# Eighteen units of w2 loaded by expert in 32 KB rows and multiplied two experts at a time, with the last steps rearranged

## The reference

```python
def moe(x, router_w, router_b, w1, b1, w2, b2):
    ...
    acc = jnp.zeros_like(xt)
    for e in range(N_EXPERTS):                      # 32
        gu = xt @ w1[e] + b1[e]                     # (288, 1024) @ (1024, 2048)
        gate = jnp.minimum(gu[:, :D_FF], SWIGLU_LIMIT)
        lin = jnp.clip(gu[:, D_FF:], -SWIGLU_LIMIT, SWIGLU_LIMIT)
        glu = gate * jax.nn.sigmoid(SWIGLU_ALPHA * gate)
        out = (glu * (lin + 1.0)) @ w2[e] + b2[e]   # (288, 1024) @ (1024, 1024)
        acc = acc + combine[:, e:e + 1] * out       # combine: top 4 of 32, else zero
    return acc.reshape(shp)

y_prompt = rmsnorm(hp, final_norm_g)
y_sample = rmsnorm(hs, final_norm_g)
```

## Time and profile before

| | |
|---|---|
| Median of three runs | 1020.77 us (1020.28 to 1022.32) |
| Profiled execution | 1020.11 us |
| Its span, first to last instruction | 1018.4 us |
| PE busy | 950.4 us (93%) |
| DVE, ACT, POOL busy | 295.8, 167.2, 74.5 us |
| Mean granted PE clock | 0.987 |
| Moved by DMA | 420.60 MB, mean 413 GB/s |

### The profile page before, as it was taken

How to read it: one execution, slowest core, us unless ns; L and a number is a source line. 1 busy time by engine, 2 the same in 40 slices (tenths; PEclk the granted TensorE clock), 3 DMA queues, 4 the chain that set the end, 5 groups by cost and what they waited for, 6 DMA issues and landing times.

```text
span 1018.4 us, 12840 instructions
## 1 busy us (share of the span) xinstructions
PE 950.4 (93%) x5422; PEld 427.7 (42%) x5422; DVE 295.8 (29%) x517; ACT 167.2 (16%) x354; POOL 74.5 (7%) x62
## 2 busy tenths in 40 slices
PE   8999999999998998989899898889899899998996
PEld 7999444343332433333243333324243334343332
DVE  5897622131312122221212222121312213131212
ACT  5355612011010101011020101002010101010012
POOL 5986000000000000000000000000000000000000
PEclk9999999999999999999999999999999999999998
DMA  9979999999999999999999999999999999999994
GB/s 321 325 296 424 368 423 432 433 426 433 425 436 425 437 432 426 432 425 434 428 434 431 431 432 424 438 423 436 427 433 431 425 438 421 434 424 434 421 419 182
DMA packets 31584, 420.60 MB, mean 413 GB/s; under 512 B 4262, under 2 KB 5062, under 8 KB 12721
## 3 DMA queue, kind: packets, MB, share of 16 engines
q1 hardware_dynamic: 31083, 418.97, 97.5%
q10 hardware_dynamic: 462, 1.10, 0.3%
HBM read 418.75 MB, written 1.49 MB: 413 GB/s over the span
## 4 chain that ended last, share of the span: by engine, by line
issue 89%; PE 9%; DMA 1%; DVE 0%; ACTq 0%; POOLq 0%; POOL 0%; DVEq 0%
PE psum L787 2%; PE psum L788 2%; PE psum L789 2%; PE psum L821 1%; PE psum L820 1%; PE psum L819 1%; DMA rows_all<-in_x_sample 1%; PE psum L706 0%; PE psum L775 0%; PE psum L796 0%; PE psum L698 0%; POOLq L86 0%; POOL rms L1982 0%; PE psum L849 0%; PE psum L765 0%
## 5 line engine op out<-in xcount | busy, mean ns | idle before, releaser
L997 PE MATMUL psum<-ring,rows_all 128*64 128x512 f32 x2012 | 460.9, 607 | 41.0 <-DMA ring<-in_exp_w 40.6
L997 PEld LDWEIGHTS psum<-ring,rows_all 128*64 128x64 f32 x2012 | 138.9, 139 | 317.8 <-issue 258.6
L1014 PE MATMUL psum<-ring,rows_all 128*64 128x512 f32 x896 | 198.0, 595 | 12.2 <-DMA ring<-in_exp_w 12.2
L1014 PEld LDWEIGHTS psum<-ring,rows_all 128*64 128x64 f32 x896 | 67.2, 137 | 134.1 <-issue 134.1
L1436 ACT ACTIVATE rows_all<-rows_all 128x512 f32<-128x512 f32 x32 | 20.1, 630 | 528.8 <-DVE rows_all L1791 528.8
L1808 DVE SCALAR_TENSOR_TENSOR y_low<-psum,gate_of,y_high 128x512 fp32r<-128x512 f32 x32 | 23.7, 751 | 243.3 <-ACT y_high L1444 243.1
L1791 DVE TENSOR_SCALAR rows_all<-psum 128x512 f32<-128x512 f32 x32 | 22.1, 692 | 196.2 <-PE psum L997 196.2
L1780 DVE TENSOR_TENSOR rows_all<-rows_all,psum 128x512 f32<-128x512 f32 x56 | 36.0, 684 | 121.1 <-PE psum L1064 121.1
L1984 POOL TENSOR_TENSOR rms<-rms,half 128x3 f32<-128x3 f32 x1 | 0.8, 849 | 910.0 <-DVE rms L1931 910.0
L1444 ACT ACTIVATE y_high<-psum,gate_of 128x512 fp32r<-128x512 f32 x32 | 22.0, 688 | 214.6 <-PE psum L1014 188.1
L890 PEld LDWEIGHTS psum<-place,x_thirds 128*128 128x128 bf16 x744 | 46.6, 97 | 13.0 <-issue 13.0
(11 more groups left out here) (270 smaller groups left out, 764.6 us busy)
## 6 DMA issues: line engine op xcount, KB each, us to landing
ring<-in_exp_w SPq DMA_DIRECT2D x53, 4096.0 KB, 30.5
ring<-in_exp_w SPq DMA_DIRECT2D x72, 2048.0 KB, 25.4
ring<-in_exp_w SPq DMA_DIRECT2D x18, 1024.0 KB, 25.6
ring<-in_w_in SPq DMA_DIRECT2D x3, 2048.0 KB, 19.8
ring<-in_w_out SPq DMA_DIRECT2D x1, 4096.0 KB, 13.0
ring<-in_exp_w SPq DMA_DIRECT2D x2, 1536.0 KB, 17.7
ring<-in_exp_w SPq DMA_DIRECT2D x5, 512.0 KB, 19.8
held<-in_exp_w SPq DMA_DIRECT2D x1, 2048.0 KB, 11.8
```

The costliest lines, as they stand in the source:

```text
L997: last = mm(psum[c * SLOTS:(c + 1) * SLOTS, bank, :], gathered_t[:, 4 * kk + j, e, :], weights, start=False, stop=(kk == 1 and j == 3), sk ...
L1014: last = mm(psum[e * SLOTS:(e + 1) * SLOTS, 4 + c, :], h_t[:, 4 * i + j, e, :], ring_w2[:, slot, e, j, c * BANK:(c + 1) * BANK], start=Fal ...
```

## The change

It has two parts.

**w2 of pairs 1 to 9.** A unit now holds all 1024 rows of one expert instead of half the rows of both. `load_wide` brings it in one transfer of 4 MB, eight rows (32 KB) in a row for each partition. The product takes both units together: `wide_product` waits for both, goes through eight steps j with both experts in each, and raises `used` by two at its end. Since a wide unit raises its landing counter by 16 instead of 32, PE adds the other 16. The hidden rows must lie eight rows to a partition: `activate` stores with `run=8`, and `turn_wide` turns them in 32 products of 64 columns with the identity in place of eight transposes. Pairs 0 and 10 to 15 stay as they were, so the loops run to `WIDE` = 5 instead of 6, and the turn h = 5 is written out behind them on each engine.

**The end.** Three of the four seeds (3, 0, 1) are written by ACT (`write_seed`) instead of multiplied by PE; PE waits for them once, before the last pair's product. The gain is loaded once, as rows of 1024 for all partitions, and not before the last unit's third part has landed; the four small transfers go. The samples' square moves from ACT to DVE. PE then turns the samples from 128 x 256 to 32 x 1024 (eight records), DVE scales them out of PSUM in two steps instead of one, and ACT stores 32 rows of 4 KB.

```diff
+            def load_wide(pair, e, slot):
+                rows = exp_w2[0][bass.ds(pair * 2 + e, 1)].rearrange("e (p j) n -> p (e j n)", j=8)
+                nc.sync.dma_start(ring_flat[:, slot], rows).then_inc(landed[slot], 16)
...
+                    elif wide:
+                        load_wide(pair - 1, i, slot)
...
-                with nc.sync.Fori(1, HALF - 2) as m:
+                with nc.sync.Fori(1, WIDE) as m:
                     h = reg(nc.sync, r * HALF + m, ROUNDS * HALF)
-                    load_period(h, 0, m * 2)
-                    load_period(h, 1, m * 2 + 1)
+                    load_period(h, 0, m * 2, wide=True)
+                    load_period(h, 1, m * 2 + 1, wide=True)
+                h5 = reg(nc.sync, r * HALF + WIDE, ROUNDS * HALF)
+                load_period(h5, 0, WIDE * 2, wide=True)
+                load_period(h5, 1, WIDE * 2 + 1)
...
-            load_last(reg(nc.sync, more * HALF + HALF, ROUNDS * HALF))
+            h8 = reg(nc.sync, more * HALF + HALF, ROUNDS * HALF)
+            load_last(h8)
+            sp.wait_ge(third_landed, 4 * h8)
             nc.sync.dma_start(gain_final, final_norm_g[None, :].to_broadcast([P, D])).then_inc(g_final_landed, 16)
-            for q in range(4):
-                nc.sync.dma_start(gain_samples[q * NS:(q + 1) * NS],
-                                  final_norm_g[None, q * QUARTER:(q + 1) * QUARTER].to_broadcast([NS, QUARTER])
-                                  ).then_inc(g_final_landed, 16)
...
+            def turn_wide(h, b, bank=6):
+
+                for e in range(2):
+                    pe.wait_ge(h_ready, 4 * h + 2 * b + e - 1)
+                    for j in range(8):
+                        for a in range(2):
+                            own = slice(a * SLOTS, (a + 1) * SLOTS)
+                            last = mm(psum[own, bank + e, j * SLOTS:(j + 1) * SLOTS],
+                                      gate_act[:, e, j * SLOTS:(j + 1) * SLOTS], ident[:, own],
+                                      start=True, stop=True, skip_group_check=True)
+                    last.then_inc(h_t_ready, 1)
...
+            def wide_product(h, b, at_unit):
+
+                slots = [(at_unit + e) % UNITS for e in range(2)]
+                pe.wait_ge(h_t_read, 4 * h + 2 * b)
+                for e in range(2):
+                    pe.wait_ge(landed[slots[e]], arrivals(h, at_unit + e) - 16)
+                for j in range(8):
+                    for c in range(YN):
+                        for e in range(2):
+                            last = mm(psum[e * SLOTS:(e + 1) * SLOTS, 4 + c, :], h_t[:, j, e, :],
+                                      ring_wide[:, slots[e], j, c * BANK:(c + 1) * BANK],
+                                      start=False, stop=(j == 7), skip_group_check=True)
+                        if j < 2 and c == 0:
+                            last.then_inc(landed[slots[j]], 16)
+                        if j == 7 and c < YN - 1:
+                            last.then_inc(y_ready, 1)
+                last.then_inc(used, 2)
...
-                        if final:
-                            seed(3)
                         turn_back(h, b)
...
-                if end:
-                    seed(0)
                 half_product(h8, h_t, 1, 1, 1, 4)
                 pe.wait_ge(h_t_read, 4 * h8)
                 add_b2(h8, 0, y_bank=0)
-                if end:
-                    seed(1)
+                pe.wait_ge(seeds_written, 3 * h8)
                 half_product(h8, h_t_last, 2, 0, 0, 0)
...
-                    pe.wait_ge(squares, FIRST_SQUARES + LAST_ORDER.index(SAMPLES) + 1)
+                    pe.wait_ge(samples_squared, 1)
...
+                    for q in range(4):
+                        last = mm(psum[0:NS, q // 2, (q % 2) * QUARTER:(q % 2 + 1) * QUARTER], ident[:, q * NS:(q + 1) * NS],
+                                  samples_acc, start=True, stop=True, skip_group_check=True)
+                    last.then_inc(samples_turned, 1)
...
+            def write_seed(j):
+
+                c, t = TILES[j]
+                A(psum[:, LAST_BANKS[j], :], x_acc[:, t, c * BANK:(c + 1) * BANK], ACT.Copy).then_inc(seeds_written, HALF)
...
-                    act.wait_ge(last_added, 1)
-                    A(work[:, 2, 0:QUARTER], samples_acc, ACT.Square, scale=D ** -0.5,
-                      accum_out=sumsq[:, 2, 2:3]).then_inc(squares, 1)
                     continue
...
-            act.wait_ge(final_dve, 3)
-            nc.scalar.dma_start(y_sample.rearrange("b t (q n) -> q (b t) n", q=4), samples_out).then_inc(stored, 16)
+            act.wait_ge(final_dve, 4)
+            nc.scalar.dma_start(y_sample.rearrange("b t n -> (b t) n"), samples_out).then_inc(stored, 16)
...
+                dve.wait_ge(last_added, 1)
+                V.scalar_tensor_tensor(out=work[:, 2, 0:QUARTER], in0=samples_acc, scalar=1.0 / D, in1=samples_acc,
+                                       op0=ALU.mult, op1=ALU.mult, accum_out=sumsq[:, 2, 2:3]).then_inc(samples_squared, 1)
...
-            V.scalar_tensor_tensor(out=samples_out, in0=samples_acc, scalar=rms[:, 2, 2:3], in1=gain_samples,
-                                   op0=ALU.mult, op1=ALU.mult).then_inc(final_dve, 1)
+            dve.wait_ge(samples_turned, 1)
+            for c in range(YN):
+                own = slice(c * BANK, (c + 1) * BANK)
+                V.scalar_tensor_tensor(out=samples_out[:, own], in0=psum[0:NS, c, :], scalar=rms[0:NS, 2, 2:3],
+                                       in1=gain_final[0:NS, own], op0=ALU.mult, op1=ALU.mult).then_inc(final_dve, 1)
```

More of the change, by code:

```diff
@@ L563, in load_first, with load_period @@
                     load_w1(pair, i, i)
-            def load_period(h, b, pair, last=False, kept=False, half=False):
+            def load_period(h, b, pair, last=False, kept=False, half=False, wide=False):
                 first = 4 if b else -2
@@ L1081, in spread_tile, with period @@
                 return_rows(b, j, 6 + j % 2, True, True).then_inc(spread, 1)
-            def period(h, b, first=False, spreads=True, final=False, kept=None, half=None):
+            def period(h, b, first=False, spreads=True, final=False, kept=None, half=None, wide=False):
                 direct = first and isinstance(h, int)
@@ L1091, in period @@
                     pe.wait_ge(gt_read, 16 * h + 8 * b)
-                if not (first or second):
+                if wide:
+                    turn_wide(h, b)
+                elif not (first or second):
                     turn_hidden(h, b)
@@ L1444, in high_y, with period @@
                     A(y_high[:, c, :], psum[:, y_bank + c, :], ACT.Copy, scale=gate_of[:, 1 - b:2 - b]).then_inc(y_high_ready, 1)
-            def period(h, b, first=False, final=False):
+            def period(h, b, first=False, final=False, wide=False):
                 second = isinstance(h, int) and h + b == 1
@@ L1484, in round_of @@
                 period(h0, 1)
-                with nc.scalar.Fori(1, HALF - 2) as m:
+                with nc.scalar.Fori(1, WIDE) as m:
                     h = reg(nc.scalar, r * HALF + m, ROUNDS * HALF)
-                    period(h, 0)
-                    period(h, 1)
+                    period(h, 0, wide=True)
+                    period(h, 1, wide=True)
+                h5 = reg(nc.scalar, r * HALF + WIDE, ROUNDS * HALF)
+                period(h5, 0, wide=True)
+                period(h5, 1)
                 h6 = reg(nc.scalar, r * HALF + HALF - 2, ROUNDS * HALF)
@@ L1810, in low_y, with period @@
                                            op1=ALU.subtract).then_inc(y_low_ready, 1)
-            def period(h, b, pair, first=False, spreads=True, final=False):
+            def period(h, b, pair, first=False, spreads=True, final=False, wide=False):
                 at_first = 12 * h + (5 if b else 1 if first else -1)
@@ L1829, in period @@
                     V.tensor_copy(pick_b2[:], picked(pair - 1)).then_inc(picked_b2, 1)
-                activate(h, b, 12 * h + (8 if b else 4 if first else 2))
+                activate(h, b, 12 * h + (8 if b else 4 if first else 2), run=8 if wide else 4)
                 if final:
```

61 lines of the change are left out of this document (42 added, 19 removed).

## The result

The changed kernel takes 1026.09 us (median of six runs, 1024.76 to 1027.86), the kernel before beside it 1020.91 (six runs, 1020.11 to 1022.32). The ratio is 1.0049, 95% interval 1.0040 to 1.0059: 5.1 us slower, where the prediction had 1.2 us faster and a range that ended at 1021.7. The profiled execution took 1025.95, with a span of 1024.2 for 1018.4 before, and a mean granted clock of 0.976 for 0.987.

What follows compares the result with a forecast made beforehand. Weight transfers were taken to bound the loop. The terms -1.3 (rows) + 0.9 (code) + 0.1 (clock) - 0.2 (sums) - 0.7 (samples' store) gave about -1.2 us, so 1019.6 against 1020.77, range 1017.3 to 1021.7.

Steps and rivals of the forecast that it cites:

- What bounds the kernel: Steady loop: weight transfers set the period of 58.44 us; PE needs 51.60 and has 6.84 to spare.
- w2 in rows of 32 KB: w2 loads of nine pairs: one 4 MB transfer for two of 2 MB gains 0.14 us a pair, 1.3 in all.
- Both experts together: Joint wait and release of two w2 units: SP issues later, but the queue stays covered, 2.9 us left, cost nothing.
- A starved queue: Rival, SP's wait behind the wide product: queue runs dry nine times, some 85 us, or 1038 at 2 us a pair; chance 0.05.
- turn_wide: PE's turning of the hidden rows: 2.2 us, 1.2 more than the eight transposes, nothing on the path.
- Code out of the loop: A pair of periods written out behind the loop: some 4.5 more instruction loads, +0.9 us, from 0 to 2.1.
- The end: Behind the loop: DVE closes the sums 0.2 us sooner, the samples' store gains 0.7, a fallen clock costs 0.1.
- the clock's 0.1: At the end, PE's longer idle before 997.39 may lower its clock: 0 to 0.9 us lost, taken as 0.1.
- the whole 2.3 us: Last stretch, samples' store on 16 engines instead of 4: by the rule alone 2.3 us would go; 0.7 was taken.
- The sum: Whole kernel: all terms together about -1.2 us, giving 1019.6 us against 1020.77.

Runs made afterwards that it cites:

- e5: The changed kernel with the last four of the wide product's eight steps left out (results not the layer's): 1019.90 us, beside 1020.84 before.
- e6: The changed kernel with the third w1 unit loaded in two halves, the first issued halfway through the wide product: 1021.14 us, beside 1020.84 before.
- e8: The changed kernel with 14 small identity products before each wait for the two wide units: 1020.38 us, beside 1020.84 before.
- e7: e6 with the loops rolled up again and pairs 1 to 11 wide: 1020.85 us, beside 1020.84 before.
- e9: e8 with the loops rolled up again and pairs 1 to 11 wide: 1022.53 us, beside 1021.18 before.
- e4: The changed kernel with 40 small identity products before each wait for the two wide units: 1060.88 us, beside 1021.27 before.
- e2: The kernel before with only the turn h = 5 written out behind the loop on every engine: 1021.75 us, beside 1021.27 before.
- e3: The kernel before with only the change's end part (seeds, gain, samples): 1019.96 us, beside 1021.27 before.
- e1: The kernel before, 16 KB rows kept, with the two w2 units waited for and freed together in ten pairs: 1026.40 us, beside 1021.27 before.
- e10: e1 with 14 small identity products ahead of each wide product: 1022.64 us, beside 1021.18 before.
- e11: The changed kernel with the wide product done expert by expert, each unit waited for and freed alone: 1069.08 us, beside 1021.21 before.

## Why the prediction was wrong

- **What bounds the kernel** held: the transfers. e5 and e6 change PE's work or its release and the period goes to 58.3 and no further.
- **w2 in rows of 32 KB** held as a rate: e5's and e8's periods are 58.28 for 58.44. In no whole time has it been seen. The parts of e8 sum to -1.3 + 0.5 - 1.3 = -2.1, measured -0.5; e6 and e7 fall short of what was expected by 1.1 and 2.0. In e8 the two places above would explain it. In e6 the trace shows one late landing among the wide pairs (681.28, by 1.0 us, with an instruction load at 670.8 and the queue full); the rest, and e7's median, stay open. The prediction also read the slices of the earlier trace rows as agreeing with the ceiling that it cites; slices of 436 to 438 GB/s are above that, by less than 1%, and the best whole period here, 25.17 MB in 58.28 us or 432 GB/s, is under it.
- **Both experts together** is the step that failed, and within it the sentence "So the cover holds and the wait costs nothing, with 2.9 us left". Three things were too small in it or not in it at all. The product was taken as at most 15.6 us; it is 15.3 to 16.8 after idles of 3.3 to 7.2, where the prediction had only seen an idle of 2.63. The way into an emptying queue was taken as 0.87 us, from a small store at rest; e9 shows 2.6 until the unit lands, and e4 2.5 to 3.9 with instruction loads among them. With these two the margin is 19.4 - 16.8 - 2.6 = 0.0 to 19.4 - 15.3 - 2.6 = 1.5 us, where the prediction had 2.9. And the queue was thought of as one thing that runs dry when its last unit lands. Its 16 engines run dry earlier: in e4 no row begins in the last 1.6 us ahead of the landing. In place of "the wait costs nothing" after loses 1.0 us a period, and e8, with a product of 13.95, none of it from its second wide period on.
- The rival *A starved queue* named the place, the mechanism and the factor nine, and its threshold was mis-sized: a product longer than 18.5 us. By e8 against after it is between 14 and 15.3. Its price was mis-sized as well: it counted on a clock that stays low through the product (28 us, 85 us in all), or on 2 us a pair. Measured were a product longer by 1.4 to 2.8 and 1.0 us a period.
- **turn_wide** was to take 2.2 us; it takes 2.09. It stands behind the product's release, so SP doesn't wait for it.
- **Code out of the loop**: +0.9 forecast, +0.5 measured (e2), in its bounds. One load taken by itself may be dearer than the 0.47 us that was its worst: 1.2 in e8, if the load at 771.7 is what made 778.56 late.
- **The end**: -0.8 forecast with the clock's 0.1, -1.3 measured (e3), in its bounds. What part of it is the samples' store was not measured by itself. By the Trainium skill's rule ("DMA: Bandwidth & Descriptors", Why a DMA increments its semaphore by 16 and not by 1), by which the whole 2.3 us would go, more was to be had than came. e3's windows, with 0.06 and 0.00 where before had 0.29 and 0.13, point its way.
- **The sum**, with e1's +5.1 for the second step and the rows at their -1.3: -1.3 + 5.1 + 0.5 - 1.3 = +3.0, measured +5.1. Without the rows' gain it is +4.3. (e1 has ten joint pairs, after nine.) The rest of 0.8 to 2.1 us is within what the intervals of the four ratios allow (each about 1 us either way).

What stays open: why the delay is so uneven in after. An issue 3.7 us ahead of the landing cost 1.3 us in one period; in the next, 2.8 us ahead (484.66, behind the product that began at 468.18), it cost nothing. In e1, too, issues 2.6 to 3.6 us ahead cost nothing in four periods and 0.7 or 1.2 in three others. Instruction loads are not the reason between 310 and 660 us, as after's queue view has none there. How far the 16 engines are out of step just then may decide; no run here shows it.

## What to carry to other kernels

A ring that is released later has to be judged by the time between the issue and the moment the queue would be empty, and this margin needs the start-up of a full transfer on all 16 engines, not the first bytes of a small one: here 5.2 us between issue and the last landing in flight were enough every time (e8), 2.4 to 3.9 mostly not (after). Whoever merges two waits also makes the engine behind them idle longer at one place, and its next work slower; both go into the same margin. Small products that keep it busy help in the long waits and do harm where the wait is short (e4, and the way in of e8). A longer loop body can bring instruction loads into the loop (e4). Before splitting or joining loads by another index, look at which products alternate on the matrix engine because of it.

## What the runs showed of the hardware that was not expected

- A 4 MB transfer issued into a queue just run dry lands 12.3 us behind its issue (e9) where units in a full queue follow each other in 9.71. In e4, where instruction loads stand between, it is 12.2 to 13.6: first rows begin 1.0 us behind the issue and take some 2 us for 1.21.
- An idle of 3.3 to 7.2 us brings TensorE's granted clock down in after (0.57 in the mean over 408.60 to 412.00, so mostly 1.2 GHz; 1.00, 2.4 GHz, in the 4 us behind) and costs the following 13.95 us of products 1.4 to 2.8; 3.39 us of small products in the gap avoid it where at most 1.7 us of idle is left (e8), and not always where 2.2 to 2.6 is left (e10: three products of ten took 15.65). Nor is the idle's length all: 3.07 us cost nothing in e1 (the product at 231.70), 2.58 cost 1.7 in e6 (at 233.01).
- 64 records of 64 columns each take 13.95 us when they alternate between two halves of the array and 26.02 when they don't (e11).
- One 16 KB instruction load, a packet of about 1 us, stands beside a landing that is 1.2 us late while the engines move 434 GB/s (e8, 778.56). Five more such loads cost 0.5 us in all (e2, an interval that includes zero).
